# A two-block transformer kernel in split fp32: the split weights' buffers begin 48 bytes in front of the moving tiles' place modulo 2048

## The reference

```python
p = h @ w_in                                   # 1024 -> some 3600 columns
x = x + mixed @ w_out                          # 1024 -> 1024
u = causal_dwconv(h @ w_up, conv_w) + conv_b   # 1024 -> 2 * 2816
x = x + (silu(gate) * up) @ w_down             # 2816 -> 1024
h = h + (gate_b * conv3(gate_c * val)) @ conv_w_out
h = h + swiglu_ffn(rms_norm(h), w13, w2)       # twice, 1024 -> 2 * 2816 -> 1024
h = h + causal_attention(...) @ mla_w_o
```

## Time and profile before

| | |
|---|---|
| runs of the kernel | 1861.69, 1863.00, 1863.84 us; median 1863.0 |
| the profiled execution's own time | 1863.52 us |
| its span, first to last instruction | 1861.7 us |
| mean granted TensorE clock | 0.997 of full |
| PE busy | 1823.8 us, 98% of the span |
| DVE, ACT, POOL busy | 49%, 38%, 11% |
| DMA | 161.03 MB, mean 86 GB/s |

### The profile page before, as it was taken

One profiled execution on the slowest core, in us unless ns is written; L12 is line 12 of the kernel. 1 busy time (PEld: TensorE's weight loads), 2 busy tenths in 40 slices (PEclk: granted clock), 3 DMA queues, 4 the chain that ended last, 5 costly groups with the idle time before them and its releaser, 6 DMA issues.

```text
span 1861.7 us, 27365 instructions
## 1 busy us (share of the span) xinstructions
PE 1823.8 (98%) x10063; PEld 1477.7 (79%) x10063; DVE 916.6 (49%) x1277; ACT 716.0 (38%) x1059; POOL 209.3 (11%) x181
## 2 busy tenths in 40 slices
PE   7999999999999999999999999999999999999998
PEld 6787776678888888888888888888776878888887
DVE  6453586557767633445544444333666343434222
ACT  6444435454444322322433232223555332323222
POOL 0030001121111110000211111101000211111110
PEclk9999999999999999999999999999999999999999
DMA  6301112133333333333333333333220233332331
GB/s 193 91 25 47 47 47 80 35 91 98 94 100 92 95 94 105 91 102 92 100 91 101 93 98 95 97 94 102 73 83 1 80 90 100 92 101 87 95 102 66
DMA packets 309228, 161.03 MB, mean 86 GB/s; under 512 B 12688, under 2 KB 306832, under 8 KB 309024
## 3 DMA queue, kind: packets, MB, share of 16 engines
q1 hardware_dynamic: 308080, 157.28, 29.2%
q0 software_dynamic: 640, 2.17, 0.3%
q10 hardware_dynamic: 432, 0.52, 0.1%
HBM read 157.85 MB, written 2.10 MB: 86 GB/s over the span
## 4 chain that ended last, share of the span: by engine, by line
PE 93%; DVE 3%; ACT 2%; issue 1%; DMA 1%; POOL 0%; ACTq 0%; POOLq 0%; DVEq 0%
PE ps L372 28%; PE ps L374 28%; PE ps L373 28%; PE ps L1765 1%; PE ps L1181 1%; PE ps L2061 1%; PE ps L2062 1%; PE ps L1497 1%; PE ps L1756 1%; PE ps L1441 1%; PE ps L922 1%; PE ps L1092 1%; DVE xlo L446 0%; PE ps L1485 0%; POOL ssq L563 0%
## 5 line engine op out<-in xcount | busy, mean ns | idle before, releaser
L372 PE MATMUL ps<-xhi,whi 128*128 128x512 f32 x1656 | 654.2, 395 | 4.0 <-DVE wlo L367 2.3
L374 PE MATMUL ps<-xhi,wlo 128*128 128x512 f32 x1656 | 645.4, 390 | 0.0
L373 PE MATMUL ps<-xlo,whi 128*128 128x512 f32 x1656 | 645.2, 390 | 0.0
L359 ACT ACTIVATE whi<-raw 128x1024 fp32r<-128x1024 f32 (+2 forms) x297 | 309.0, 1040 | 707.6 <-PE ps L374 707.1
L367 DVE TENSOR_TENSOR wlo<-raw,whi 128x1024 fp32r<-128x1024 f32 (+2 forms) x297 | 365.4, 1230 | 275.7 <-ACT whi L359 275.7
L372 PEld LDWEIGHTS ps<-xhi,whi 128*128 128x128 f32 x1656 | 311.2, 188 | 72.6 <-issue 4.2
L373 PEld LDWEIGHTS ps<-xlo,whi 128*128 128x128 f32 x1656 | 311.4, 188 | 65.9 <-issue 2.9
L374 PEld LDWEIGHTS ps<-xhi,wlo 128*128 128x128 f32 x1656 | 311.1, 188 | 65.1
L622 DVE TENSOR_TENSOR zS<-ps,rs 128x512 f32<-128x512 f32 x132 | 91.3, 692 | 297.1 <-PE ps L374 284.5
L374 PE MATMUL ps<-h_hi,wlo 128*128 128x512 f32 x528 | 205.4, 389 | 0.0
L372 PE MATMUL ps<-h_hi,whi 128*128 128x512 f32 x528 | 205.4, 389 | 0.0
(11 more groups left out here) (333 smaller groups left out, 1484.7 us busy)
## 6 DMA issues: line engine op xcount, KB each, us to landing
raw<-in_conv_ffn_w SPq DMA_DIRECT2D x52, 512.0 KB, 3.8
raw<-in_mla_ffn_w SPq DMA_DIRECT2D x52, 512.0 KB, 3.8
raw<-in_w_up SPq DMA_DIRECT2D x44, 512.0 KB, 3.8
raw<-in_w_in SPq DMA_DIRECT2D x28, 512.0 KB, 3.8
raw<-in_conv_w_in SPq DMA_DIRECT2D x24, 512.0 KB, 3.7
raw<-in_w_down SPq DMA_DIRECT2D x16, 448.0 KB, 3.7
raw<-in_conv_ffn_w SPq DMA_DIRECT2D x16, 448.0 KB, 3.7
raw<-in_mla_ffn_w SPq DMA_DIRECT2D x16, 448.0 KB, 3.8
```

Source lines behind the costliest of these rows:

```text
L359: a.activation(whi[:, u % PARTS, 0:n], raw[:, u % RAW, 0:n], ACT.Copy).then_inc(hi_split, 1)
L372: t_.matmul(out, wh, xh, start=first, stop=False)
L373: t_.matmul(out, wh, xl, start=False, stop=False)
L374: return t_.matmul(out, wl, xh, start=False, stop=last)
```

## The change

The two buffers become slices of one. It begins where `whi` began, at the common place modulo 2048. 500 elements (2000 bytes) are left free, then come the two halves of 2 x 1024 elements each, then 12 free elements (48 bytes). 2000 bytes are 2048 - 48, so `whi` begins 48 bytes in front of the place that the moving tiles have, and `wlo`, 8192 bytes on, as well. The buffer is 18432 bytes a partition, 9 x 2048, where the two were 16384, so all that comes after it stays where it was modulo 2048. Nothing else is changed: no instruction, size, order or wait.

```diff
@@ -250,8 +250,10 @@
         xhi = sb("xhi", [P, KT, T], F32R)
         xlo = sb("xlo", [P, KT, T], F32R)
         raw = sb("raw", [P, RAW, UNIT])
-        whi = sb("whi", [P, PARTS, UNIT], F32R)
-        wlo = sb("wlo", [P, PARTS, UNIT], F32R)
+        ahead, parts = 500, PARTS * UNIT
+        whi_wlo = sb("whi_wlo", [P, ahead + 2 * parts + 12], F32R)
+        whi, wlo = (whi_wlo[:, ahead + n * parts:ahead + (n + 1) * parts].rearrange("p (b u) -> p b u", u=UNIT)
+                    for n in range(2))
         cst = sb("cst", [P, NCONST])
```

## The result

| | before | after |
|---|---|---|
| median of the runs | 1863.4 us (4 runs) | 1902.2 us (4 runs, 1900.8 to 1906.1) |
| ratio | | 1.0208, 95% interval 1.0196 to 1.022 |
| profiled execution, span | 1863.5, 1861.7 us | 1906.1, 1904.3 us |
| PE busy | 98% | 98% |
| ACT waits for the last reader of its buffer | 707.1 us | 740.9 us |

38.8 us more, against 46 us less that were forecast. The count of instructions is the same (27365). The mean granted clock is 0.997 in the profiled execution before and 0.995 in the one after, which has some 8 us more at the lower level (twice 0.5% of 1904 us, against twice 0.3% of 1862) and is the longest of its four; the 1902.2 us of the median don't rest on it.

What follows compares the result with a forecast made beforehand. The prediction took PE, busy 98%, to be bound by the pitch of 6948 split matmuls. From 1863.5 us it took 46.6 us (6948 x 6.7 ns) to get 1816.9, forecast as 1817 us, range 1788 to 1888.

Steps and rivals of the forecast that it cites:

- about 3 ns of hand-over and about 10 ns of disputed reads: Split passes, lines 372 to 374: the 13.3 ns a matmul above 213.3 ns, read as weight load and stream meeting.
- a halving of the excess: Split passes: the change takes the pitch between matmul starts from 226.7 to 220.0 ns; chance 0.34.
- 6948 x 6.7 ns = 46.6 us saved: All split matmuls, lines 372 to 374: gain from a pitch of 220.0 instead of 226.7 ns.
- The rival "no effect": Split passes: fixed hand-over at full clock, or loads settle to the same relation; time stays 1863 us; chance 0.22.
- the 231 ns of the earlier trace: Split passes behind an interruption: nine pitches of 231.1 ns each, then back to 226.7; taken to show pitch varies.
- The bound, the count of 6948 and the pitch as the only thing that moves: PE, busy 98%: 6948 split matmuls at 226.7 ns make 1575 us; only that pitch can move more than a few us.
- Only the place modulo 512 or less matters: Weights' 128-column blocks, 512 bytes each: starts stand 0.68 us apart through four k, so larger distances make no difference.
- The splits' writes and the DMA: Splits on ACT and DVE at the moved place: costed at nothing, within 10% of a duration; loads still covered.
- The values of the latent attention: Second attention, 48 matmuls with split weights as moving tile: 10 ns more or less each, 0.5 us.
- The bound from above: Split passes: if every matmul were like those behind an interruption, 231.1 ns, a loss of 31 us.
- The worse half that was left out: Part of the slower case beyond the range's end at 1888 us; with a little below, less than 2 in 10.
- The rival "slower": Split passes: place -48 lets no settled relation form, or one with more meetings; 231.1 ns, 1894 us; chance 0.23.

Runs made afterwards that it cites:

- the repeats at 256 and 272: Weights' buffers 256 and 272 bytes in front of the moving tiles' place, against 0 in the kernel before: 1865.2 us (1.0007) and 1871.0 us (1.0041).

## Why the prediction was wrong

The step that failed is the reading of the 13.3 ns above the ideal stream as "about 3 ns of hand-over and about 10 ns of disputed reads", and with it the choice of 220.0 ns, a halving of the excess. The 3 ns came from the plain fp32 products, and the split passes were taken to have the same hand-over. They don't: theirs is 13.3 ns for 256 as for 512 columns, and neither a quarter of the load nor a load from one address makes it less. 226.7 ns was the floor in all that was tried, and none of the ten other places won anything. So the term 6948 x 6.7 ns = 46.6 us saved should have been a loss of 41.2 us.

The text had what it needed for this. The rival "no effect" names the floor: the pitch falls back to 226.7 after each interruption. I held the 231 ns of the earlier trace rows against it, as if both could not be true. They are two things: a fixed price of 13.3 ns, and above it an extra by the rhythm, nothing at the best place and up to 6.7 ns in the mean at others.

By its other steps:
- The bound, the count of 6948 and the pitch as the only thing that moves: right. Nearly the whole change stands in lines 374 to 376 of the new kernel, 41.2 of 42.6 us. That the pitch would be the same in all stages wasn't right: 233.33 ns in ffn2, 231.9 in ffn3 up.
- Only the place modulo 512 or less matters, and only relative to the moving tiles: right, and it is 256 (the run with everything moved, by 32 bytes; the repeats at 256 and 272).
- The splits' writes and the DMA: no sign of a price; the splits' medians are within 1 ns of the earlier trace rows.
- The values of the latent attention, where the split weights are the moving tile: their distances went from 228.2 to 232.3 ns in the mean. The price comes there too, some 0.2 us in all, within the 0.5 that the prediction allowed.
- The bound from above, 231.1 ns from the stretch after an interruption, was too low. The mean is 232.87 after, and other places gave 233.3. The range ended at 1888, short of this rival's own 1894. The worse half that was left out is where the result lies.
- The rival "slower" had mechanism and place right (no settled relation at 226.7). Its price was 31 us for 39. It was given 0.23; the argument for it, that the present relation is the smallest pitch at full clock, was what the rows showed best.
- The rule of the Trainium skill, "TensorE: Matmul & The Clock Gate", Part 2, that loading weights takes nothing from the running matmul: measured, 32 columns of load instead of 128 give no shorter pitch, which agrees with it. It has no place for what the weights' address does: by it the time would have stayed at 1863, and it is 1902.2.

What stays open: what in the chip makes the rhythm. The runs show that it changes with the place modulo 256, with the width of the load and product, with what the load reads, and in the changed kernel between stages; they don't show the resource. Whether the sums in one PSUM bank or the moving tile's own place have a part in it wasn't tried. No version was faster than the kernel before.

## What to carry to other kernels

Before you move an operand, find out whether the present pitch is already the floor. Half-length matmuls tell in one run which part of the pitch goes by column and which comes once with each matmul and its load. A perfectly even pitch over hundreds of matmuls is a state that can be lost: every change of place that was tried, but the one by 256 bytes, and a narrower matmul in one pass of three cost 0.4 to 2.4% here. In a kernel bound by such a chain, try stationary and moving operands of fp32r products at the same place modulo 256 bytes, and look at the distances one by one, not at a mean duration.

## What the runs showed of the hardware

- Split (fp32r) matmuls at the 2.4 GHz level, each with its own load of 128 columns and in the best rhythm, cost columns / 2.4 ns + 13.3 ns: 226.67 ns with 512 and 120.0 ns with 256 columns. At the 1.2 GHz level the same passes take 426.7 ns, with nothing on top.
- The settled rhythms close, to the resolution of the records, on whole multiples of 6.67 ns: 226.67 (34), 233.33 (35), three matmuls in 686.7 (103, 64 in front), four in 913.3 (137, 16 in front), nine in 2087 (313, the change). 13.3 ns is two of them. Longer ones that the other traces show do so too: twelve in 2800 ns (420, 96 in front) and 21 in 4880 ns (732, 128 in front). That is arithmetic on rhythms, not a shown mechanism.
- Less can be slower: 32 weight columns and 32 rows of product instead of 128 cost 1.5% at the place 0, and loads whose 128 columns are one address cost 1.2%.
